# A transformer layer pair on one core: latent projections on the undivided input, one bias-line product, and a reordered entry

## The reference

```python
h = concatenate([meta, x])                   # 16 + 256 tokens, d = 1024
n = _rms_norm(h, attn_norm)                  # h * rsqrt(mean(h*h) + 1e-6) * gain
proj = n @ w_in                              # c_q 256, c_kv 256, k_rope 32, dq 512, dk 512, dv 512
q  = _rms_norm(c_q,  q_norm)  @ w_uq         # 8 heads of 96
kv = _rms_norm(c_kv, kv_norm) @ w_ukv        # 8 heads of 64 + 64
...
bias = bias_table[_t5_bucket(q_pos[:, None] - pos[None, :])]   # 32 buckets x 4 heads, differential attention
```

## Time and profile before

| what | value |
|---|---|
| median of 3 runs | 1433.87 us |
| profiled execution, its own time | 1428.98 us |
| its span | 1426.8 us |
| PE busy | 1388.3 us, 97% |
| DVE, ACT, POOL busy | 979.6, 678.9, 700.0 us |
| mean memory traffic | 175 GB/s |

### The profile page before, as it was taken

How to read it: one execution, slowest core, us unless ns; L and a number is a source line. 1 busy time by engine, 2 the same in 40 slices (tenths; PEclk the granted TensorE clock), 3 DMA queues, 4 the chain that set the end, 5 groups by cost and what they waited for, 6 DMA issues and landing times.

```text
span 1426.8 us, 28445 instructions
## 1 busy us (share of the span) xinstructions
PE 1388.3 (97%) x9878; PEld 1252.6 (88%) x9878; DVE 979.6 (69%) x1676; ACT 678.9 (48%) x1034; POOL 700.0 (49%) x347
## 2 busy tenths in 40 slices
PE   7999998999999999999999999999999989999997
PEld 6777688999999999988888888999989967899996
DVE  4524658999988888866666666544455755699996
ACT  4433654445455555543333333444455456555554
POOL 4313257778766666644444444444422535344541
PEclk9999999999999999999999999999999999999999
DMA  7321135567755555567777777555553524355552
GB/s 291 123 86 40 36 129 203 190 199 215 214 181 184 180 183 183 178 207 238 231 236 238 227 239 226 178 190 190 178 174 132 177 66 127 121 189 185 182 177 74
DMA packets 89852, 249.67 MB, mean 175 GB/s; under 512 B 10032, under 2 KB 35904, under 8 KB 89152
## 3 DMA queue, kind: packets, MB, share of 16 engines
q1 hardware_dynamic: 85968, 237.67, 51.7%
q10 hardware_dynamic: 3824, 11.17, 2.1%
HBM read 233.56 MB, written 15.24 MB: 174 GB/s over the span
## 4 chain that ended last, share of the span: by engine, by line
PE 80%; DVE 16%; ACT 2%; issue 1%; POOL 0%; DMA 0%; ACTq 0%; DVEq 0%
PE ps L1830 37%; PE ps L2251 25%; PE ps L2238 4%; PE ps L2221 3%; DVE big L1458 2%; DVE big L1455 2%; DVE big L1474 1%; PE ps L1845 1%; PE ps L2059 1%; DVE big L1175 1%; PE ps L2101 1%; DVE big L1461 1%; PE ps L2079 1%; PE ps L2029 1%; DVE ps L1496 1%
## 5 line engine op out<-in xcount | busy, mean ns | idle before, releaser
L540 POOL TENSOR_TENSOR w_lo<-raw,w_hi 128x1024 fp32r<-128x1024 f32 x258 | 640.8, 2486 | 611.9 <-ACT w_hi L655 607.6
L1830 PE MATMUL ps<-x_op,w_hi 128*128 128x256 f32 (+1 forms) x3888 | 723.8, 287 | 8.3 <-POOL w_lo L540 1.9
L1830 PEld LDWEIGHTS ps<-x_op,w_hi 128*128 128x128 f32 x3888 | 606.6, 191 | 22.4 <-issue 9.4
L1830 PE MATMUL ps<-x_op,w_lo 128*128 128x256 f32 (+1 forms) x1944 | 550.2, 283 | 0.0
L655 ACT ACTIVATE w_hi<-raw 128x1024 fp32r<-128x1024 f32 x399 | 419.2, 1054 | 264.6 <-PE ps L2251 206.7
L1830 PEld LDWEIGHTS ps<-x_op,w_lo 128*128 128x128 f32 x1944 | 371.6, 191 | 0.0
L2251 PE MATMUL ps<-w_hi,h_op 128*128 128x512 f32 x1008 | 280.7, 396 | 0.0
L1151 DVE TENSOR_TENSOR w_lo<-raw,w_hi 128x1024 fp32r<-128x1024 f32 x140 | 181.3, 1295 | 98.7 <-ACT w_hi L655 98.1
L2251 PEld LDWEIGHTS ps<-w_hi,h_op 128*128 128x128 f32 x1008 | 187.5, 188 | 43.3 <-issue 0.2
L2251 PE MATMUL ps<-w_lo,h_op 128*128 128x512 f32 x504 | 158.6, 395 | 0.0
L1525 DVE TENSOR_TENSOR work<-route_t,ps 128x1536 bf16<-128x1536 bf16 x64 | 112.3, 1754 | 8.7
(11 more groups left out here) (306 smaller groups left out, 1258.0 us busy)
## 6 DMA issues: line engine op xcount, KB each, us to landing
raw<-blocks SPq DMA_DIRECT2D x403, 512.0 KB, 3.6
early_store<-kv_mem SPq DMA_DIRECT2D x96, 128.0 KB, 1.7
work<-early_store SPq DMA_DIRECT2D x96, 128.0 KB, 3.6
big<-consts ACTq DMA_DIRECT2D x2, 1336.0 KB, 6.2
big<-h_t ACTq DMA_DIRECT2D x4, 272.0 KB, 3.8
big<-bias_lines ACTq DMA_DIRECT2D x8, 136.0 KB, 2.6
bias_lines<-route_t ACTq DMA_DIRECT2D x4, 264.0 KB, 2.2
res<-mem_t SPq DMA_DIRECT2D x1, 1024.0 KB, 8.1
```

The costliest lines, as they stand in the source:

```text
L540: pool.tensor_tensor(w_lo[:, s, :], raw[:, s, :], w_hi[:, s, :].bitcast(F32), ALU.subtract).then_inc(sem("lo_pool"), 1)
L1830: mm = pe.matmul(ps[:, m_bank, 0:T], w, xp, start=(k == 0 and j == 0), stop=(k == last and j == 2))
```

## The change

1. **Latents on the undivided input.** Blocks 0 to 3 are multiplied with `in_op`, the input times gain, split into high and low part, without the division by the root. ACT makes the high parts, DVE the low parts, directly from the input. In `undivided_in` the products with `w_hi` come first, for each tile as it gets ready, then those with `w_lo`. Block 4 on use the normalised input as before (`UNDIVIDED_IN = 4`). The latent sums get a third product each, ones with `eps_r2` = 2e-6 * r * r which the sum over 128 partitions turns into 256 times 1e-6 * r * r, in place of the bias 1e-6 in the root. The latent roots get storage of their own (`lat_r`), `lat_sq` moves to `spare`.
2. **The input's norm** is computed beside the products: POOL squares two quarters and ACT two, POOL and DVE fold eight tiles to two, and PE sums two products instead of eight, behind block 1. ACT takes the root behind the high parts of blocks 3 and 4. The warm-up products stand at the very start of PE's list.
3. **The memory's norm:** POOL folds the eight squares to two; the sum is two products and stands behind block 5, its root behind the query evacuations, the multiplication by DVE behind the latents. PE waits for that root in front of the value products, which use the same bank.
4. **Bias lines:** one product makes all four lines on four partitions; they are stored once, and one DMA repeats each line 128 times within `scratch`. It and the bias loads are issued by SP, between loads of blocks.
5. **Order:** block 0 is loaded at once, blocks 1 to 3 behind the second quarter; the constants, `w_uq`, `w_ukv` and `mem_t` move to SP's queue, between blocks; the low part of block 0 goes from POOL to DVE; the memsets of the head buffers `q_full` and `k_full`, whose memory `in_op` now uses, move behind block 3.

```diff
@@ lo_owner
+    if n == 0:
+        return "dve"
@@ SP
-            sp.wait_ge(sem("h_loaded2"), 16)
-            for j in range(RING):
+            load(At(0))
+            sp.wait_ge(sem("h_loaded1"), 16)
+            for j in range(1, RING):
                 load(At(j))
-            sp.dma_start(flat2(mem_t[:, :, :]), dram["mem_t"]).then_inc(sem("mem_loaded"), 16)
+            sp.dma_start(rel_in, dram["rel_bias"]).then_inc(sem("rel_loaded"), 16)
+            sp.dma_start(cst, dram["consts"][:, N_CONSTS_KEPT:]).then_inc(sem("cst_loaded"), 16)
+            sp.dma_start(kept[:, :], dram["consts"][:, 0:N_CONSTS_KEPT]).then_inc(sem("kept_loaded"), 16)
             for n in range(RING, B_EARLY + LOADS_AHEAD):
                 next_load(At(n))
+                if n == RING:
+                    sp.dma_start(flat2(w_uq), dram["w_uq"]).then_inc(sem("wu_loaded"), 16)
+                if n == RING + 1:
+                    sp.dma_start(flat2(w_ukv), dram["w_ukv"]).then_inc(sem("wu_loaded"), 16)
+                if n == RING + 2:
+                    sp.dma_start(flat2(mem_t[:, :, :]), dram["mem_t"]).then_inc(sem("mem_loaded"), 16)
+                if n == RING + 5:
+                    sp.wait_ge(sem("line_stored"), 16)
+                    sp.dma_start(scratch[:, 0:P], scratch[:, P:P + 1].to_broadcast([DH, P, LINE])).then_inc(sem("line_stored"), 16)
+                if RING + 8 <= n < RING + 8 + DH:
+                    h = n - RING - 8
+                    sp.wait_ge(sem("line_stored"), 32)
+                    for t in range(2):
...
+                        sp.dma_start(bias[:, h, t, :], src).then_inc(sem("bias_loaded"), 16)
@@ POOL
+            for c in range(2):
+                at = slice(2 * c * NK, 2 * (c + 1) * NK)
+                pool.wait_ge(sem(f"h_loaded{c}"), 16)
+                pool.tensor_tensor(sq[:, at], flat2(h_t)[:, at], flat2(h_t)[:, at], ALU.mult).then_inc(sem("in_squares"), 1)
+            pool.wait_ge(sem("in_squares"), 2)
+            pool.tensor_tensor(sq[:, 0:2 * NK], sq[:, 0:2 * NK], sq[:, 2 * NK:4 * NK], ALU.add).then_inc(sem("in_squares"), 1)
...
-            pool.memset(flat2(q_full), 0.0)
-            pool.memset(flat2(k_full), 0.0)
-            los(B_IN, B_IN + 1)
+            los(B_IN, B_IN + 5)
             norm_lo(R_ATTN, NK)
-            los(B_IN + 1, B_IN + 9)
+            pool.wait_ge(sem("block_used"), UNDIVIDED_IN)
+            pool.memset(flat2(q_full), 0.0)
+            pool.memset(flat2(k_full), 0.0).then_inc(sem("heads_zero"), 1)
+            los(B_IN + 5, B_IN + 7)
+            pool.wait_ge(sem("rms_squares"), KT * (R_MEM + 1))
...
+            los(B_IN + 7, B_IN + 9)
@@ ACT
             for c in range(4):
                 act.wait_ge(sem(f"h_loaded{c}"), 16)
-                squares(flat2(h_t)[:, 2 * c * NK:2 * (c + 1) * NK], 2 * c, NK, 2)
-            root(R_ATTN, NK)
+                for k in range(2 * c, 2 * c + 2):
+                    act.activation(in_op[:, 0, k, :], h_t[:, k, :], ACT.Copy, scale=pcol("attn", k)).then_inc(sem("in_hi"), 1)
+                if c == 0:
+                    his(1)
             his(2)
...
+            evacuate_in(0)
+            his(B_IN + 5)
+            root(R_ATTN, NK)
+            evacuate_in(1)
+            lat_squares(0)
+            act.activation(eps_r2, rt, ACT.Square, scale=math.sqrt(2 * EPS)).then_inc(sem("eps_r2"), 1)
+            norm_hi(R_ATTN, NK, 0, range(0, 2))
+            evacuate_in(2)
+            norm_hi(R_ATTN, NK, 0, range(2, 5))
+            lat_root(0)
+            norm_hi(R_ATTN, NK, 0, range(5, KT))
+            evacuate_in(3)
+            lat_squares(1)
+            lines_out()
+            evacuate_in(4)
+            lat_root(1)
+            squares(flat2(mem_t[:, :, :]), 0, NQ, KT)
+            evacuate_in(5)
+            act.wait_ge(sem("q_product"), 1)
+            act.activation(flat2(q_mla), ...)
+            act.activation(xf[0:QK, 0:HEADS * NQ], ...)
+            act.activation(mem_rt, ps[:, 3, 0:NQ], ACT.Sqrt, scale=1.0 / D, bias=E_MODEL).then_inc(sem("rms_root"), 1)
             evacuate_in(6)
@@ DVE
+                for k in range(2 * c, 2 * c + 2):
+                    dve.wait_ge(sem("in_hi"), k + 1)
+                    dve.scalar_tensor_tensor(out=in_op[:, 1, k, :], in0=h_t[:, k, :], scalar=pcol("attn", k),
+                                             in1=in_op[:, 0, k, :].bitcast(F32), op0=ALU.mult, op1=ALU.subtract).then_inc(sem("in_lo"), 1)
+                if c == 2:
+                    los(1)
+            los(2)
...
@@ PE
             pe.wait_ge(sem("ones_set"), 1)
-            norm(R_ATTN, NK)
             keep_warm(20, 5)
...
+            undivided_in(0)
+            undivided_in(1)
+            pe.wait_ge(sem("squares_folded"), 1)
+            for k in range(2):
+                mm = pe.matmul(ps[:, 2, 0:NK], ones[:, :], sq[:, k * NK:(k + 1) * NK], start=(k == 0), stop=(k == 1))
+            mm.then_inc(sem("rms_sum"), 1)
+            undivided_in(2)
+            latent_sum(0)
+            undivided_in(3)
+            relative_lines()
             project_in(4)
-            pe.wait_ge(sem("rms_root"), R_MEM + 1)
             latent_sum(1)
...
             project_in(5)
+            pe.wait_ge(sem("lat_root"), 2)
+            pe.wait_ge(sem("mem_squares"), 2)
+            for k in range(2):
+                mm = pe.matmul(ps[:, 3, 0:NQ], ones[:, :], sq[:, k * NQ:(k + 1) * NQ], start=(k == 0), stop=(k == 1))
+            mm.then_inc(sem("rms_sum"), 1)
             project_in(6)
+            pe.wait_ge(sem("rms_root"), R_MEM + 1)
             pe.wait_ge(sem("lat_ready"), 2)
             values(0)
```

More of the change, by code:

```diff
@@ L100 @@
 N_CONSTS_KEPT = 2 * 128
+Q_FULL = 21682
+UNDIVIDED_IN = 4
 def taken(n):
@@ L678, in root, with norm_hi @@
                 act.activation(rt[:, 0:T], ps[:, bank, 0:T], ACT.Sqrt, scale=1.0 / D, bias=E_MODEL).then_inc(sem("rms_root"), 1)
-            def norm_hi(r, T, n):
+            def norm_hi(r, T, n, tiles=range(KT)):
                 if n:
                     act.wait_ge(sem("block_used"), n)
-                for k in range(KT):
+                for k in tiles:
                     act.wait_ge(sem("rms_xf"), normed(r) + k + 1)
@@ L791, in _ @@
-            evacuate_in(6)
-            act.wait_ge(sem("line_stored"), 16 * DH)
-            for h in range(DH):
-                for t in range(2):
-                    start = FAR - N_META - P * t
-                    src = skewed[h, start:start + P * (LINE - 1)].rearrange("(p j) -> p j", j=LINE - 1)[:, 0:NK]
-                    act.dma_start(bias[:, h, t, :], src).then_inc(sem("bias_loaded"), 16)
+            evacuate_in(6)
             evacuate_in(7)
@@ L1160, in los, with norm @@
                     ahead[0] += 1
-            def norm(r, src, gain, T, operand=True, between={}):
-                dve.wait_ge(sem("rms_root"), r + 1)
-                step(dve.reciprocal(rb[:, 0:T], rt[:, 0:T]))
+            def norm(r, src, gain, T, operand=True, between={}, inverted=False):
+                if not inverted:
+                    inverse_root(r, T)
                 def lower(k):
@@ L1888, in project_in, with undivided_in, relative_lines @@
                 n, m = B_IN + j, M_IN + j
-                project(At(n), m % 2, NK, bank_free(m), operand(R_ATTN) if j == 0 else None, tiles)
-            def relative_line(h):
-                if h:
-                    pe.wait_ge(sem("line_ready"), h)
+                project(At(n), m % 2, NK, bank_free(m), operand(R_ATTN) if j == UNDIVIDED_IN else None, tiles)
+            def undivided_in(j):
+                n, m = At(B_IN + j), M_IN + j
+                if j == 0:
+                    pe.wait_ge(sem("hi_done"), 1)
+                else:
+                    arrived(n)
+                if bank_free(m) is not None:
+                    pe.wait_ge(*bank_free(m))
+                out, s = ps[:, m % 2, 0:NK], n.mod(RING)
+                for k in range(KT):
+                    if j == 0:
+                        pe.wait_ge(sem("in_lo"), k + 1)
+                    for part in range(2):
+                        pe.matmul(out, w_hi[:, s, k * P:k * P + P], in_op[:, part, k, :], start=(k == 0 and part == 0), stop=False)
+                if j == 0:
+                    arrived(n)
+                for k in range(KT):
+                    mm = pe.matmul(out, w_lo[:, s, k * P:k * P + P], in_op[:, 0, k, :], start=False, stop=(k == KT - 1))
+                mm.then_inc(sem("block_used"), 1)
+            def relative_lines():
+                pe.wait_ge(sem("rel_loaded"), 16)
+                pe.wait_ge(sem("cst_loaded"), 16)
                 for a, e, b in ((0, LINE // 2, 4), (LINE // 2, LINE, 5)):
-                    mm = pe.matmul(ps[:, b, 0:e - a], rel_rep[:, h, :], con("bucket", BUCKETS, cst)[:, a:e], start=True, stop=True)
+                    mm = pe.matmul(ps[0:DH, b, 0:e - a], rel_in, con("bucket", BUCKETS, cst)[:, a:e], start=True, stop=True)
                 mm.then_inc(sem("line_done"), 1)
```

123 lines of the change are left out of this document (53 added, 70 removed).

## The result

Four executions of the changed kernel took 1415.68 to 1417.08 us, median 1415.76; four of the kernel before, beside them, 1433.55 to 1433.94. The ratio is 0.9885, 95% interval 0.9865 to 0.9905: 18.0 us faster, where 11.4 were forecast. The profiled execution of the changed kernel took 1415.72, its span 1413.8.

The account below looks back on a forecast made before the run. PE was taken to bound the kernel, busy 1388.3 of 1426.8 us. Block 4 ending 14.6 us earlier, less 3.2 more up to block 7, saves 11.4: 1433.87 - 11.4 = 1422.5 us, 8-in-10 range 1419 to 1427.5.

Parts of the forecast that it names:

- I take the saving from the span and subtract it from the median: Final sum: the 11.4 us saved, counted in the profiled span of 1426.8, is taken off the runs' median 1433.87.
- the normalising of eight tiles: Input's norm before block 4: 8.6 us as before, plus 0.9 for ACT's evacuation and latent root; last tile at 30.5.
- Block 4 landed at 17.5: Block 4's load, queued behind blocks 1 to 3 and the constants on SP, was to land at 17.5 us.
- The root was to be done at 19.1: ACT's input root, behind block 4's high part, done at 19.1 us; the reciprocal, 1.86 us, then at 21.0.
- The locks on POOL's account: Block 0: POOL's three operations, 1.2 to 1.35 us each, could serialise with DVE's low parts, to 14.1 us at worst.
- The latent sum's wait of 0.9: Behind block 4: PE waits 0.9 us for ACT's block 5 high part, evacuation and squares before the second latent sum.
- PE in front of the values: Before the value products, PE waits for the memory root behind two query evacuations: 0.9 us left uncovered.
- The repeat of the lines: The DMA copying each bias line 128 times in memory: 2.5 us at full rate, 20 at most, hidden, counted zero.
- block 0 slow: Rival, chance 0.20: sparse block 0 products drop PE's clock, block 1 takes 2.4 us more; saving 8.2, time 1425.7.
- The early end: Rival, chance 0.15: constants flow faster, POOL falls between DVE's operations, root at 17; saving 14 us, time 1419.9.
- Slower: Rival, chance 0.04: the bias lines' copy drains so slowly that block 10's load is late; time 1474.
- no change: Rival, chance 0.04: a wait behind block 7, such as a late normalised memory input, takes the whole saving; time 1433.9.

Follow-up runs that it names:

- the kernel with the middle filled: The kernel before plus 16 extra 128-column products between second-layer attention steps where PE waits for POOL: 12 executions, 1429.44 to 1435.29 us.
- with the middle filled too: The kernel before with warm-up products in front of the input's sum and 16 extra products in the second layer: 1429.55 to 1431.69 us, median 1430.66.
- The root-first run: The changed kernel with the input's root in front of block 4's high part on ACT instead of behind it: median 1416.99 us, ratio 0.9906.
- four line products: The changed kernel with the bias-line product made four times at the same place instead of once: median 1422.14 us, ratio 0.9944.

## Why the prediction was wrong

The mechanism was right: PE's first blocks no longer wait, the norm's chain runs beside them, the saving reaches the end unchanged. Two things were off.

**The step that failed** is the sentence "I take the saving from the span and subtract it from the median". The prediction had both numbers, 1428.98 and 1433.87, and took their 4.9 us to be an offset that stays. It was a cost that executions of the kernel before carry or do not carry: in the one such execution that was profiled 3.5 us by block 2, most of it block 1 on the lower clock, and 1.4 near 240 us. Moving the warm-up products, which the change does, removes it. From 1428.98 the same 11.4 lead to 1417.6, with both ends of the range 4.9 lower, 1414.1 to 1422.6, and 1415.76 within. The whole miss is 6.7 us: 4.9 of this kind, 1.25 at block 7, 0.35 behind it, and the last 0.2 because the changed kernel's own time is 1.9 over its span and not 2.2. That the first runs' 1433.55 to 1433.94 were of this kind is argued, not shown: their clock is not known, but 28 executions at 0.995 took 1433.24 to 1434.20, and the one at 0.995 above 1433 that was profiled, that of the kernel with the middle filled, had these stretches. The removal by the warm-ups' place is shown by two pairs: 10 of 23 against 0 of 12 with it alone, 7 of 17 against 0 of 12 with the middle filled too.

**A term of the sum was too large:** the normalising of eight tiles, "8.6 us" plus "0.9 in all", to 30.5. It took 21.56 to 29.06, 7.5. The 8.6 held a lock that the change takes away: in the earlier trace rows DVE's first two products took 2.08 us, beside a low part of POOL from 13.25 on; here POOL's low part was over at 21.73 and the first two took 0.92. The root-first run puts the lock back and has its 1.3 us again. And ACT's evacuation and latent root fitted between the tiles at no cost. Block 4 thus ended at 29.8 instead of 31.0, and that 1.2 is all of the difference at block 7: from there on the forecast's sum was 23.55, measured 53.31 - 29.8 = 23.5, its terms off by up to 0.5 each and cancelling. Ahead of the normalising the forecast was 0.5 too early.

Point by point:

- Block 1 at 12.7 to 15.4: 13.76. Block 4 landed at 17.5: 18.18. The root was to be done at 19.1 and the reciprocal at 21.0: 19.63 and 21.5.
- The locks on POOL's account were smaller: its three operations took 1.09, 1.09 and 1.34 and were over at 8.9, before DVE's first low part at 10.3.
- The latent sum's wait of 0.9 was 0.39, and its products 1.64 instead of 1.4. PE in front of the values: 0.9 forecast, 0.93 measured. This is the wait that stayed in the kernel.
- The repeat of the lines was hidden, as taken. It was issued at 32.53. The trace has no landing for it, but SP issued the first bias load, which waits for it, at 50.30, directly behind block 12's load, and block 10's high part was not late (54.94). So it took at most 17.8 us. The Trainium skill, DMA: Bandwidth & Descriptors, "Why a DMA increments its semaphore by 16 and not by 1", would give 10.2, an estimate from the prediction; no run here shows whether it is so.
- *Rival "block 0 slow"* had the right mechanism in the wrong kernel. In the changed one the lower clock fell on block 0's own end in some traces (12 to 15 us) and cost about 1 us at the sum, not 3.2, since the products there are few and the norm waits for weights too. The argument against it, that block 1 had run at full pace in before, rested on one execution; another of that kernel's kind had 5.81. *"The early end"*, 1419.9 by 14 us, was nearest in time for the wrong reason: neither the constants nor the root came earlier.
- *Slower* and *no change* had nothing on their side.

What stays open: why the stretch near 1150 to 1170 us comes in some executions and not in others of the same kernel. It costs 3.8 to 4.0 us in either kernel. Whether an edit at the head changes how often it comes is not shown; with four line products all six executions were 5.8 us slower or more, 1.8 of it explained by block 7. Open too is why PE's wait for DVE near 377 us is, but for one trace, there only when the clock did not fall near 230 us.

## What to carry to other kernels

Where a kernel is bound by PE at 97%, look at how its executions scatter before you subtract a saving from a median: if the profiled one lies outside the heap that the median is in, profile one of that heap too, ask which stretch it has that the first did not, and whether the change touches it. Look for thin products directly in front of dense ones: there the dense ones pay for the lower clock (5.81 us instead of 3.29), and here it helped to put the warm-up products at the very start, which moved the slow time to where PE waits anyway. And when a duration is taken from a row, look at what ran beside it; a 2.08 that held a lock is a 0.92 when the neighbour has gone.

## What the runs showed of the hardware

- The granted clock fell to the lower level inside a busy kernel, each time behind thin products: at 12 to 32 us (block 0), near 225 or 237 us (1.4 to 1.5 us, made up for at the wait for DVE in all traces but one), and from 1146 or 1159 us on, for about 10 us. The changed kernel had 47 products in the 10 us in front of the second place (215 to 225) and 27 in the 6 us in front of the third (1140 to 1146), where later, in dense work, it had 44 in 5 us. The Trainium skill, TensorE: Matmul & The Clock Gate, "Terms", puts the penalty at half of the time at the lower level, which would be some 5 us for the last, an estimate from 10.2 us at that level in the second trace of the kernel before. The traces say 3.8: PE was busy for 7.56 of 9 us there at full clock and for 8.42 at half, so a part of it went into pauses.
- Whether a stretch comes is not fixed by the program: the kernel before has the last one in one of its two traces and not in the other. Of 23 executions of the same kernel on the same chip 13 took 1428.14 to 1431.00 at a mean granted clock of 0.996 to 0.999, and 10 took 1432.23 to 1434.20 at 0.993 to 0.995.
- 20 float32 warm-up products of 128 columns, 40 instructions, took 6.13 to 7.68 us at the very start of the traces; in the kernel before, behind the sum, 4.6. The granted clock is 1.00 in both places, so that number alone does not show the slow start.
- DVE and POOL beside each other in the changed kernel:

```profile
53.10 4.75 POOL L643 TENSOR_TENSOR big<-big 96x2048 f32<-96x2048 f32 x1 [3.19 <-issue]
53.45 7.82 DVE L1186 TENSOR_TENSOR w_lo<-raw,w_hi 128x1024 fp32r<-128x1024 f32 x1
57.79 2.39 POOL L570 TENSOR_TENSOR w_lo<-raw,w_hi 128x1024 fp32r<-128x1024 f32 x1
```

  DVE's low part of 1024 columns, 1.21 alone, took 7.82: it ended 1.1 behind the second of POOL's two operations, and these ran as long as elsewhere (4.58 and 2.35). The Trainium skill, SBUF — State Buffer, "Who interferes with whom", calls this an exclusive lock; the trace agrees.
